# Sample output parts with the queries stationary: four sequences on four output strips, and two products that turn the result back

## The reference

```python
inter = jnp.einsum('bhtk,bhkv->bhtv', qc, S) * q_dec          # retention
num = jnp.einsum('bhts,bhsv->bhtv', s, vc) + w_prev[..., None] * jnp.einsum('bhtk,bhkv->bhtv', qc, C)   # mLSTM
inter = jnp.einsum('bhtk,bhkv->bhtv', qc * jnp.exp(A), S)     # HGRN2
```

## Time and profile before

| | us |
|---|---|
| median of 3 runs | 1495.98 (1495.96 to 1498.33) |
| profiled execution, its own time | 1493.7 |
| span of that execution | 1491.9 |
| TensorE busy in the span | 1463.3 (98%) |
| VectorE busy | 1152.4 (77%) |
| ScalarE busy | 932.5 (63%) |
| mean granted TensorE clock | 0.998 |

### The profile page before, as it was taken

The page is one execution under the profiler, slowest core; times in us unless marked ns, Lnnn a source line. Parts: engine busy times, 40 slices in busy tenths (PEclk is TensorE's granted clock), DMA queues, the critical chain, the costliest instruction groups (busy, mean ns, idle before and its releaser), DMA issues.

```text
span 1491.9 us, 22989 instructions
## 1 busy us (share of the span) xinstructions
PE 1463.3 (98%) x8445; PEld 1298.7 (87%) x8445; DVE 1152.4 (77%) x1307; ACT 932.5 (63%) x971; POOL 89.4 (6%) x96
## 2 busy tenths in 40 slices
PE   9999999999999989999999999999999999999997
PEld 8899889999999979998788888888888888888885
DVE  5766688455456697777898888989889898898887
ACT  5344655433333764353777878778787787877875
POOL 1023110000001000120300000000000000000011
PEclk9999999999999999999999999999999999999999
DMA  8577725996446523542999999999999999999994
GB/s 232 145 130 141 137 89 164 303 294 194 134 142 181 165 92 123 151 128 62 407 405 389 391 359 395 378 385 387 362 400 372 386 389 359 397 378 383 394 343 168
DMA packets 213732, 404.04 MB, mean 271 GB/s; under 512 B 13487, under 2 KB 130507, under 8 KB 213534
## 3 DMA queue, kind: packets, MB, share of 16 engines
q1 hardware_dynamic: 203120, 373.62, 71.9%
q0 software_dynamic: 6320, 22.20, 5.0%
q10 hardware_dynamic: 4222, 7.26, 1.3%
HBM read 372.75 MB, written 30.28 MB: 270 GB/s over the span
## 4 chain that ended last, share of the span: by engine, by line
PE 90%; DVE 7%; ACT 2%; issue 1%; POOL 0%; ACTq 0%; DVEq 0%; POOLq 0%
PE bank L530 27%; PE bank L531 26%; PE bank L532 26%; PE bank L764 2%; PE bank L1198 1%; DVE dense_lo L1937 1%; PE bank L806 1%; PE bank L709 1%; PE bank L1022 1%; PE bank L756 1%; ACT dense_hi L1426 0%; PE bank L697 0%; PE bank L1125 0%; DVE w_lo L2438 0%; PE bank L717 0%
## 5 line engine op out<-in xcount | busy, mean ns | idle before, releaser
L2438 DVE TENSOR_TENSOR w_lo<-arena,w_hi 128x2048 fp32r<-128x2048 f32 (+1 forms) x280 | 596.9, 2165 | 80.8 <-ACT w_hi L1775 79.7
L1775 ACT ACTIVATE w_hi<-arena 128x2048 fp32r<-128x2048 f32 (+1 forms) x280 | 502.1, 1820 | 116.1 <-PE bank L532 112.4
L530 PE MATMUL bank<-w_hi,xg_hi 128*128 128x512 f32 x704 | 275.6, 391 | 1.2 <-DVE xg_lo L2496 0.6
L532 PE MATMUL bank<-w_hi,xg_lo 128*128 128x512 f32 x704 | 274.1, 389 | 0.0
L531 PE MATMUL bank<-w_lo,xg_hi 128*128 128x512 f32 x704 | 274.0, 389 | 0.0
L1937 DVE TENSOR_TENSOR dense_lo<-ring,dense_hi 128x2048 fp32r<-128x2048 f32 (+1 forms) x77 | 165.5, 2150 | 124.5 <-ACT dense_hi L1426 124.4
L1426 ACT ACTIVATE dense_hi<-ring 128x2048 fp32r<-128x2048 f32 (+1 forms) x78 | 140.5, 1802 | 138.6 <-PE bank L532 109.8
L530 PEld LDWEIGHTS bank<-w_hi,xg_hi 128*128 128x128 f32 x704 | 132.2, 188 | 31.6 <-issue 3.1
L532 PEld LDWEIGHTS bank<-w_hi,xg_lo 128*128 128x128 f32 x704 | 132.1, 188 | 27.6
L531 PEld LDWEIGHTS bank<-w_lo,xg_hi 128*128 128x128 f32 x704 | 132.2, 188 | 26.9
L530 PE MATMUL bank<-h_hi,dense_hi 128*128 128x320 f32 x448 | 142.9, 319 | 2.6 <-DVE h_lo_a L2007 1.6
(11 more groups left out here) (471 smaller groups left out, 2361.8 us busy)
## 6 DMA issues: line engine op xcount, KB each, us to landing
arena<-in_w_moe_down SPq DMA_DIRECT2D x176, 512.0 KB, 6.9
arena<-in_w_moe_gate SPq DMA_DIRECT2D x128, 512.0 KB, 6.7
arena<-in_w_moe_up SPq DMA_DIRECT2D x128, 512.0 KB, 7.9
arena<-in_w_moe_gate SPq DMA_DIRECT2D x64, 384.0 KB, 4.2
arena<-in_w_moe_up SPq DMA_DIRECT2D x64, 384.0 KB, 5.1
ring<-in_w_in_ab SPq DMA_DIRECT2D x32, 512.0 KB, 8.6
ring<-in_w_in_c SPq DMA_DIRECT2D x32, 512.0 KB, 4.7
expert_rows<-ZERO SPq DMA_DIRECT2D x12, 1024.0 KB, 7.6
```

The source lines that it names most:

```text
L530: mm(out, left[0], right[0], start=start, stop=False)
L532: return mm(out, left[1], right[0], start=False, stop=stop)
L1775: fn(WH[SLOT_OF[p]][:, 0:unit_size(p)], STAGE[:, s, 0:unit_size(p)], ACT.Copy).then_inc(S("unit_hi"), 1)
L2438: v.tensor_tensor(WL[w][:, 0:n], STAGE[:, s, 0:n], WH[w][:, 0:n].bitcast(F32), ALU.subtract).then_inc(S("unit_split"), 1)
```

## The change

For every head a new step, thin u, stands in both lists ahead of weigh u or out u. It makes the state part of the output by itself: for each half r of the samples and each j of 4 sequences, the 32 queries of the half are stationary (128x32), the state of sequence 4r+j is the moving operand (128 columns), and the result goes to output strip j (partitions 32j to 32j+32), columns of half r, of one bank. Of a strip's 32 rows only the 8 that belong to sequence 4r+j are wanted. VectorE (layer 0) or ScalarE (layer 1) copies the 128x256 result to a new buffer TH, two deep. In `weigh` the 8 products per head are replaced by two: TH's half r is stationary (128x128) and picked columns of the identity are moving (32 columns, `to_token`), which turns the wanted rows into the 32 token columns of that half, added to the same bank as before. The waits for the queries and for the states move from weigh u or out u to thin u; weigh waits for the copy instead. A woven piece has one yield in its middle instead of four.

```diff
-    rq x0 x1 x2 x3 x4 x5 x6 x7 carry gates rk rope0 rope1 columns rv score0 score1 mq0 mq1 along weigh0 mq2 along weigh1 conv0 center0 conv1
-    silu0 mq3 state0 wh wl wh state1 conv2 wl score2 conv3 silu1 mk0 mk1 silu2 wh silu3 score3 weigh2 mk2
+    rq x0 x1 x2 x3 x4 x5 x6 x7 carry gates rk rope0 rope1 columns rv score0 score1 mq0 thin0 mq1 along weigh0 thin1 mq2 along weigh1 conv0 center0 conv1
+    silu0 mq3 state0 wh wl wh state1 conv2 wl score2 conv3 silu1 mk0 thin2 mk1 silu2 wh silu3 score3 weigh2 thin3 mk2
...
-    conv7 center1 silu7 wl mv4 score4 mv5 mo0 weigh4 wh shift5 wl mo1 state4 score5 wh center2 wl mo2
-    finish4 weigh5 finish5 center3 center4 conv_out rg0 state5 center5 var0 root0 shift6 score6 mo3 weigh6
-    mix0 mix1 wh mix2 gate0 wl rg1 shift7 finish6 score7 mix3 gate1 wh state6 mix4 mix5 wl center6 weigh7
+    conv7 center1 silu7 wl mv4 score4 mv5 thin4 mo0 weigh4 wh shift5 wl mo1 state4 score5 wh center2 wl thin5 mo2
+    finish4 weigh5 finish5 center3 center4 conv_out rg0 state5 center5 var0 root0 shift6 score6 mo3 thin6 weigh6
+    mix0 mix1 wh mix2 gate0 wl rg1 shift7 finish6 score7 mix3 gate1 wh state6 mix4 mix5 wl thin7 center6 weigh7
...
-    xend0 kend0 v0 v1 wh db1 wh xb1 wl lb0 turn0 lb1 v2 la8 v3 db2 pb1 v4 wl wh xb2 wl out0 v5 v6 pb2
-    lb2 db3 state0 turn1 v7 xb3 lb3 sq0 v8 wh pb3 out1 wl v9 turn2 db4 out2 sq1 db5 xb4 lb4 state1 v10 state2
-    pb4 db6 xb5 g0 lb5 turn3 sq2 xb6 wh v11 pb5 out3 wh wl pb6 sq3 lb6 wl g1 db7 xb7 g2 pb7 g3 lb7 end1 state3
-    xend1 wh g4 lb8 kend1 wl g5 turn4 turn5 silug0 out4 wh sq4 gate0 wl g6 along out5 sq5 gate1 state4 varc0 rootc0
-    turn6 gate2 gate3 state5 turn7 g7 along out6 sq6 silug1 silug2 mixc0 mixc1 mixc2 mixc3 state6 h0 h1 h2 h3 out7 sq7 gate4
+    xend0 kend0 v0 v1 wh db1 wh xb1 wl lb0 turn0 lb1 v2 la8 v3 db2 pb1 thin0 v4 wl wh xb2 wl out0 v5 v6 pb2
+    lb2 db3 state0 turn1 v7 xb3 lb3 sq0 thin1 v8 wh pb3 out1 wl thin2 v9 turn2 db4 out2 sq1 db5 xb4 lb4 state1 v10 state2
+    pb4 db6 xb5 g0 lb5 turn3 sq2 xb6 thin3 wh v11 pb5 out3 wh wl pb6 sq3 lb6 wl g1 db7 xb7 g2 pb7 g3 lb7 end1 state3
+    xend1 wh g4 lb8 kend1 wl g5 turn4 thin4 turn5 silug0 out4 wh sq4 gate0 wl thin5 g6 along out5 sq5 gate1 state4 varc0 rootc0
+    turn6 gate2 gate3 state5 turn7 thin6 g7 along out6 sq6 silug1 silug2 mixc0 mixc1 mixc2 mixc3 thin7 state6 h0 h1 h2 h3 out7 sq7 gate4
...
+        TH = region(15104, 2, 2, DH)
+        to_token = bass.AP(tensor=ident.tensor, offset=ident.offset, ap=[list(ident.ap[0]), [QUAD + TS, QUAD // TS], [1, TS]])
...
                     yield
-                    for s in range(NB):
-                        ins = mm(b[:, TP + s * TS:TP + (s + 1) * TS], states[:, s, :], right[:, s * TS:(s + 1) * TS],
-                                 start=False, stop=(s == NB - 1), skip_group_check=True)
-                        if s % 2 and s < NB - 1:
-                            yield
+                    after_empty(pe, right)
+                    for r in range(2):
+                        ins = mm(b[:, TP + r * QUAD:TP + (r + 1) * QUAD].rearrange("p (j t) -> p j t", t=TS), thin[:, r, :],
+                                 to_token, start=False, stop=(r == 1), skip_group_check=True)
                 close_bank(kind, ins, name)
                 yield
...
+            def thin_rows(layer, u, right):
+
                 pe.wait_ge(S(f"qe{layer}"), u // 4 + 1 if layer else u + 1)
                 pe.wait_ge(S(f"state_in_{STATE_SLOT[u]}"), 16 * state_turn(layer, u))
                 kind = "act" if layer else "dve"
                 b = open_bank(kind)
-                yield from weigh(b, values, probs, right, state_tile(layer, u), ("num", layer, u), kind)
+                for r in range(2):
+                    for j in range(4):
+                        ins = mm(b[j * QUAD:(j + 1) * QUAD, r * DH:(r + 1) * DH], right[:, r * QUAD:(r + 1) * QUAD],
+                                 state_tile(layer, u)[:, 4 * r + j, :], start=True, stop=True)
+                close_bank(kind, ins, ("thin", layer, u))
...
+                elif name == "thin":
+                    if u >= 2:
+                        after_fill(act, ("num", 1, u - 2))
+                    free(fn(TH[:, u % 2], take(("thin", 1, u))[:, 0:2 * DH].rearrange("p (r v) -> p r v", v=DH), ACT.Copy))
...
+                elif name == "thin":
+                    if u >= 2:
+                        after_fill(dve, ("num", 0, u - 2))
+                    free(v.tensor_copy(TH[:, u % 2], take(("thin", 0, u))[:, 0:2 * DH].rearrange("p (r v) -> p r v", v=DH)))
```

More of the change, by code:

```diff
@@ L752, in turn_keys, with weigh @@
                 close_bank("act", ins, ("kn", layer, u))
-            def weigh(b, left, probs, right, states, name, kind="dve"):
+            def weigh(b, left, probs, right, thin, name, kind="dve"):
                 mm(b[:, 0:TP], left(0), probs[:, 0:TP], start=True, stop=False, skip_group_check=True)
@@ L758, in weigh @@
                 mm(b[:, TP:NT], left(2), probs[:, 384:448], start=False, stop=False, skip_group_check=True)
-                if states is None:
+                if thin is None:
                     ins = mm(b[:, TP:NT], ones, right, start=False, stop=True, skip_group_check=True)
@@ L762, in weigh @@
                     yield
-                    for s in range(NB):
-                        ins = mm(b[:, TP + s * TS:TP + (s + 1) * TS], states[:, s, :], right[:, s * TS:(s + 1) * TS],
-                                 start=False, stop=(s == NB - 1), skip_group_check=True)
-                        if s % 2 and s < NB - 1:
-                            yield
+                    after_empty(pe, right)
+                    for r in range(2):
+                        ins = mm(b[:, TP + r * QUAD:TP + (r + 1) * QUAD].rearrange("p (j t) -> p j t", t=TS), thin[:, r, :],
+                                 to_token, start=False, stop=(r == 1), skip_group_check=True)
                 close_bank(kind, ins, name)
                 yield
-            def outputs(layer, u, probs, probs_ready, right):
-                values = lambda i: V[:, i, u * DH:(u + 1) * DH]
-                probs_ready()
+            def thin_rows(layer, u, right):
                 pe.wait_ge(S(f"qe{layer}"), u // 4 + 1 if layer else u + 1)
@@ L777, in outputs @@
                 b = open_bank(kind)
-                yield from weigh(b, values, probs, right, state_tile(layer, u), ("num", layer, u), kind)
+                for r in range(2):
[3 more added lines that the diff above has]
+                close_bank(kind, ins, ("thin", layer, u))
+            def outputs(layer, u, probs, probs_ready):
+                values = lambda i: V[:, i, u * DH:(u + 1) * DH]
+                probs_ready()
+                kind = "act" if layer else "dve"
+                b = open_bank(kind)
+                yield from weigh(b, values, probs, ("thin", layer, u), TH[:, u % 2], ("num", layer, u), kind)
                 if layer == 0 and u >= H4:
@@ L903, in _ @@
                 elif name == "weigh":
-                    piece_along(outputs(0, u, PB[:, u % 2, :], lambda: after_empty(pe, ("sc", 0, u)), QE[:, u % 2, :]))
+                    piece_along(outputs(0, u, PB[:, u % 2, :], lambda: after_empty(pe, ("sc", 0, u))))
+                elif name == "thin":
+                    thin_rows(0, u, QE[:, u % 2, :])
                 elif name == "state":
@@ L1069, in _ @@
                     pe.wait_ge(S("vx1"), 1)
-                    piece_along(outputs(1, u, PH[:, u, :], lambda: pe.wait_ge(S("chunks_parted"), u // 4 + 1), Q[:, u, TP:NT]))
+                    piece_along(outputs(1, u, PH[:, u, :], lambda: pe.wait_ge(S("chunks_parted"), u // 4 + 1)))
+                elif name == "thin":
+                    thin_rows(1, u, Q[:, u, TP:NT])
                 elif name == "state":
```

## The result

| | before | after |
|---|---|---|
| median, us | 1496.44 (5 runs, 1495.96 to 1498.33) | 1502.82 (5 runs, 1501.56 to 1505.36) |
| ratio | | 1.0040, 95% interval 1.0026 to 1.0054 |
| profiled execution, its own time | 1493.7 | 1501.56 |
| its span | 1491.9 | 1499.7 |
| TensorE busy in the span | 1463.3 | 1461.6 |

The kernel became 6.4 us slower, more than the 0.2% that can be told from no change. The forecast was 1.7 us slower, 1497.7 in a range up to 1502.5. The measured median lies 0.3 us above that range as it stands; by the ratio, on the median that the forecast started from, 1.0040 x 1495.98 = 1502.0 lies within it. Lines moved by a few: the three products of a projection are 533 to 535 (530 to 532 before), the values' products 759 to 761, the thin step is 781 and turning back 768.

What follows compares the result with a forecast made beforehand. TensorE was taken as the bound, 90% of the chain. 10.1 us saved over 16 heads, less 0.2, 2.8, 1.0, 3.0, 0.6, 1.95 and 2.3, made it 1.7 us slower: 1497.7 us, range 1493.5 to 1502.5.

Steps and rivals of the forecast that it cites:

- Thin and turning back: Every head on TensorE: 0.69 + 0.44 us instead of 1.76, 0.63 saved, 10.1 us over 16 heads.
- Rival (c): Thin step: strips don't overlap with these operands, a head costs 2.2 us, about 1510 us in all; chance 0.08.
- rival (d): Thin step: passes cost a quarter of 110 ns, thin takes 0.58 us, 1496.7 us in all; chance 0.08.
- Head 2: Layer 0, thin2 behind mk0: TensorE waits 2.8 us for VectorE's scaled queries.
- Head 5: Layer 0: thin5 waits 0.5 us for queries, center4 is 0.35 us later; 1.0 us less than the count.
- Head 7, layer 0: Turning back waits 2.35 us for VectorE's copy behind wl; no gain, 3.0 us less than the count.
- Head 3, layer 1: Level products behind out3 have no slack, so the saving becomes a wait: 0.6 us less.
- Head 5, layer 1: TensorE waits 1.95 us at out5 for ScalarE's copy of thin5, queued behind sq4.
- Head 7, layer 1: Thin7 waits 0.9 us for the states' load, state6 starts 1.0 us later; with head 6, 2.3 us less.
- Output projection: End of layer 1: VectorE's unbroken work up to the low parts, waited for 1.7 us, hides what out7 saves.
- Rival (a): Layer 0: head 2's queries and head 7's copy only half as late, gain comes through, 1492 us; chance 0.12.
- Rival (b): Layer 1: head 7's states land 3 to 4 us later, or a just-covered copy waits; 1501 us; chance 0.22.

Runs made afterwards that it cites:

- changed, again: The changed kernel as it is, timed a second time: 1503.18 us (6 runs), ratio 1.0043.
- before + the wait: The kernel before, with TensorE waiting ahead of mk1 in layer 0 until head 2's scaled queries are written, no thin step: 1501.66 us, ratio 1.0030.
- thin2 behind mk1: The changed kernel with thin2 of layer 0 moved from behind mk0 to behind mk1: 1499.0 us, ratio 1.0008.
- thin2's wait filled: The changed kernel with nine unused products of ones by the identity ahead of thin2's wait in layer 0: 1501.3 us, ratio 1.0030.
- thin7 early: The changed kernel with thin7 of layer 0 moved directly behind state6, so VectorE copies it ahead of its weight split: 1496.64 us, ratio 1.0003.
- layer 1 moved: The changed kernel with layer 1's thin3 moved ahead of sq2, thin5 ahead of silug0 and thin7 behind state6: 1498.6 us, ratio 1.0019.
- three waits filled: The changed kernel with unused products in the waits at layer 0's thin2 and head 7's turning back, and layer 1's head 5 turning back: 1497.66 us, ratio 1.0008.
- all moved: The changed kernel with six thin steps moved, thin2, thin5, thin7 in layer 0 and thin3, thin5, thin7 in layer 1: 1489.09 us, again 1489.67 us.
- before again: The kernel before as it is, profiled a second time: 1496.7 us (1 run), span 1494.9.

## Why the loss was 6.4 us and not 1.7: the clock's term

Each run lists its span and its mean granted clock. At half the clock a stretch of TensorE work takes twice as long, so span x (1 - clock) estimates what the lowered clock cost that run, and span x clock what it would have taken without. Two things make the last column rough: a run's clock is listed to 0.001, or 1.5 us, and the clock also falls at the very end, behind TensorE's last work, where it costs nothing (worth 1.7 to 4.1 us of the column in the profiles, 3.6 in the first of before and 2.0 in the first of changed). So only differences of means are read from it. Means over all runs of a kernel:

| kernel | runs | span x clock | lost to the clock |
|---|---|---|---|
| before (three groups of runs) | 33, 23, 15 | 1488.1, 1488.7, 1488.1 | 6.7, 5.5, 6.2 |
| changed | 5 | 1489.9 | 11.4 |
| changed, again | 6 | 1490.5 | 10.3 |
| before + the wait | 12 | 1490.6 | 8.9 |
| thin2 behind mk1 | 12 | 1488.0 | 8.6 |
| thin2's wait filled | 12 | 1489.8 | 9.4 |
| thin7 early | 11 | 1488.4 | 6.7 |
| layer 1 moved | 11 | 1485.8 | 10.9 |
| three waits filled | 11 | 1490.4 | 5.3 |
| all moved | 10, 4 | 1481.9, 1482.7 | 6.0, 4.8 |

The column without the clock holds the prediction's sum: before to changed it is 1489.9 - 1488.3 = 1.6 and 1490.5 - 1488.3 = 2.2 us, against 1.7 forecast. The last column holds the other 4 to 5 us, which no step of the prediction had. Filling three waits leaves the first as it is (1490.4) and brings the second from about 11 back to before's level (5.3), some 5.5 us less; the median is then 1497.66, by chance the very number predicted. In the profiles the three places had falls worth some 4.4 us in a mean profile with their waits empty (1.5 at head 2, 1.9 at head 7, 1.0 in layer 1). What this table can't do is a split of single runs: one kernel's runs differ by several us in the last column, as the same wait is followed by a fall in one run and by none in another.

By the prediction's steps:

- **Thin and turning back**: 0.57 and 0.42 us against 0.69 and 0.44. The extrapolation from the strip rows was 0.12 us too high; whether its 34 ns a pass or its 0.14 us for going in and out was too much, no run separates. 16 x (0.77 - 0.63) = 2.2 us too little gained, some of it under waits. Rival (c), that the strips don't overlap, is out; the value that the Trainium skill's four-fold rule (TensorEngine Tiling (Array Packing), Theoretical Speedup) gave for thin as rival (d), 0.58 us, is what came, but not that rival's time.
- **Head 0**: a wait of 0.18 us, 0.2 forecast. **Head 2**: 2.35, 2.8 forecast; part of the difference is that mk0 was taken to end at 103.65, half way, while the trace of before has mk1's first product at 103.90. **Head 5**: 0.45, 0.5 forecast, and center4 waits 0.8. **Head 7, layer 0**: 2.33, 2.35 forecast; not forecast was that thin7 also waits 0.7 us for its bank, which VectorE's instructions of line 2097 hold.
- **Head 3, layer 1**: no gain, as forecast, and more: 0.58 us for ScalarE's copy and 0.5 us of the level products behind it. **Head 5, layer 1**: 1.85, 1.95 forecast. **Head 7, layer 1**: thin7 waits 0.5, 0.9 forecast.
- **Output projection**: 1.9 us of wait for the low parts, 1.7 before, and 1.2 us for line 2168's tile, new. The experts' stretch was taken as fixed, and it is, to 0.1 us: its first product starts 7.9 us later than before, and the span is 7.8 us longer.
- **What failed** is the sum's silent term: that a wait costs what it lasts. The 1.7 us came out right for the work and the waits, in part because its errors cancelled (the heads gained 2.2 us more and the waits of head 2 and of the load were 0.85 shorter, while 0.7 us for thin7's bank, 0.6 for head 3's copy, 1.2 for line 2168 and 0.4 more of center4 were not in it); the clock's 4 to 5 us had no term, no chance and no part in the range. That the range nearly or just holds the result is luck, as its upper end was set for a late load. Each of the forecast's long waits was priced at its length, with all of TensorE behind it at full clock. At head 2 the price was 2.35 + 1.55, at head 7 2.33 + 1.68 in one profile and 2.33 + 3.17 in the other. All granted clocks of before were 1.00 at these places, and the prediction carried that level over to a kernel in which TensorE stands still there.
- **Rival (a)**, queries and copy half as late: no, both waits have their full length. **Rival (b)** gave 1501, slower, for a late load: right in sign, wrong in its mechanism, as the load made thin7 wait only 0.5 us; of its other part, a copy judged to be just covered, 0.58 us came at head 3 of layer 1. Its number was near by luck. Slower by over 0.2% had been given a chance of 0.36, for these reasons and none of the clock.

How firmly the cause is shown differs by place. At head 2 the clock fell within 103 to 112 us in all five profiles in which the 2.4 us stood empty (changed twice, before + the wait, thin7 early, layer 1 moved), and in none of the seven in which the wait was absent or filled. Behind head 7's turning back it fell in four of five with the wait: with thin2 moved it stayed at 1.00 at 206 to 212, though the wait was 2.3 us. It fell in one of seven without an empty wait there, that of before + the wait. So the wait raises the chance of a fall from low to high; it doesn't settle it, and why those two profiles went the other way is open. In layer 1 the 1.85 us wait was followed by a clock below 1.00 within 650 to 670 us in three of its five profiles (changed again, thin7 early and thin2's fill; not the first of changed or thin2 behind mk1). Behind the output projection's wait of 1.6 to 1.9 us, old and new kernels alike, it fell in five of twelve profiles (before again, changed, before + the wait, thin2 behind mk1, thin2's fill). At the router's products, short ones and around a wait of under 1 us, it fell in eleven of twelve, all but the first of before. In one of these (all moved) it began 0.9 us ahead of that wait, so the wait is not its cause there; no run changed anything at this place, and its cause is open. The excess of moving thin7 alone, 6.5 us for 3.9 expected, is explained in part: the table puts 2.1 us in the waits and 3.6 in the clock (means, 5.7 in all), and the fall at head 7 cost 3.2 us in the profile of the changed kernel on that chip. Why a fall costs once 1.7 and once 3.2 us is open.

## What to carry to other kernels

Where TensorE is at full clock throughout, don't price a wait at its length: one of 2.35 us cost 3.9 here, 5.5 at another place and time, and 2.35 with products in it that nothing reads. Before a product is moved forward in an in-order queue, write beside it when its inputs come free; six steps, put behind what they wait for, or with their copy ahead of long work in the copying engine's queue, turned 0.4% lost into 0.45% gained, and the prediction had read five of the six places from the trace of before. When a forecast's waits come out right and the time doesn't, look at the granted clock of the stretches behind them.

## What the runs showed of the hardware

- The granted clock fell behind single empty stretches of TensorE of 2.3 to 2.4 us, from 1.00 to windows of 0.50 to 0.79, and cost 1.4 to 1.7 us in six profiled places, measured against a filled or absent wait (5.59 to 5.74 us from thin2 to score3 for 4.19; 10.19 and 10.30 from head 7's turning back to center7 for 8.62), and 3.1 to 3.2 us in two (11.72 and 11.79 for 8.62). Products of ones by the identity in the gap kept it at 1.00. The Trainium skill (TensorE: Matmul & The Clock Gate, What's actually happening) says that the low rate is the default and that activity releases it; the filled waits agree. That one gap of this length, in a kernel whose TensorE is 98% busy, brings it back was seen here in nine of ten places. Gaps of 1.85 us did it in three of five, gaps of 1.6 to 1.9 at the output projection in five of twelve, and at the router's products a fall stood at or around a gap of 0.8 to 1.0 us in eleven of twelve, for a cause that no run tested.
- Sixteen passes of 128x32 on four strips with 128 columns took 0.57 us from their start to the next product's, 36 ns a pass; sixteen full passes with 8 columns took 1.76 us.
- Two profiles of the unchanged kernel differed by 3.0 us, nearly all of it behind 680 us, where the second has two falls and the first none, with the same waits.
